# K stage spread out, first matrix copy ahead of the v store, u chunk loads one per weight unit, attention halves first in the first projection step

## The reference

```python
hn = rms_norm(h, norm1_g[l])                       # h: 272 tokens x 2048
q, k, v, u, g_na, g_ssm = jnp.split(hn @ w_in[l], IN_SPLITS, axis=-1)
y_na  = neighbourhood_attention(q, k, v, rpb) @ w_proj_na[l]
y_ssm = s5_branch(u, ...) @ w_proj_ssm[l]          # scan over positions, both directions, then GLU
mixed = sigmoid(g_na) * y_na + sigmoid(g_ssm) * y_ssm
h = h + mixed @ w_out[l]
h = h + conv_gated_ffn(rms_norm(h, norm2_g[l]), w_up[l], conv_w[l], conv_b[l], w_down[l])
return rms_norm(h, final_g)[:, N_META:]
```

## Time and profile before

| what | value |
|---|---|
| median of three runs | 1484.79 us (1483.28 to 1488.35) |
| the profiled execution | 1484.02 us, of which the profile's span is 1482.3 us |
| busy: PE / DVE / ACT / POOL | 1458.3 / 589.0 / 672.0 / 1032.8 us |
| granted TensorE clock, mean | 0.994 |
| DMA, mean over the span | 187 GB/s |

### The profile page before, as it was taken

One profiled execution on the slowest core, in us unless ns is written; L12 is line 12 of the kernel. 1 busy time (PEld: TensorE's weight loads), 2 busy tenths in 40 slices (PEclk: granted clock), 3 DMA queues, 4 the chain that ended last, 5 costly groups with the idle time before them and its releaser, 6 DMA issues.

```text
span 1482.3 us, 30668 instructions
## 1 busy us (share of the span) xinstructions
PE 1458.3 (98%) x11826; PEld 1384.7 (93%) x11826; DVE 589.0 (40%) x1159; ACT 672.0 (45%) x913; POOL 1032.8 (70%) x488
## 2 busy tenths in 40 slices
PE   8999999999999999999999999999999999999997
PEld 7999999999888999999999999999999998888886
DVE  3766888888546334533322222222222222003002
ACT  5536444442344364454554444444444443334333
POOL 5500038860577778888788888888888887888885
PEclk8999999999999999999999999999999999999999
DMA  7997457654676445575565555555555556555653
GB/s 211 301 206 223 140 158 221 195 176 121 171 226 206 150 159 176 182 257 178 169 193 185 184 184 183 180 181 181 183 182 184 184 183 197 187 186 184 194 187 130
DMA packets 250495, 277.14 MB, mean 187 GB/s; under 512 B 30749, under 2 KB 236925, under 8 KB 249773
## 3 DMA queue, kind: packets, MB, share of 16 engines
q1 hardware_dynamic: 235840, 254.84, 56.2%
q10 hardware_dynamic: 14508, 21.09, 4.4%
q0 software_dynamic: 64, 0.07, 0.0%
HBM read 263.32 MB, written 12.39 MB: 186 GB/s over the span
## 4 chain that ended last, share of the span: by engine, by line
PE 87%; DVE 4%; ACT 2%; DMA 2%; SPq 1%; issue 1%; DVEq 1%; POOL 0%; ACTq 0%; POOLq 0%
PE ps L1538 22%; PE ps L1540 21%; PE ps L1539 21%; PE ps L1906 6%; PE ps L1908 6%; PE ps L1907 6%; PE ps L1748 1%; DMA w_raw<-in_w_in 1%; DVE w_lo L524 1%; ACT w_hi L520 1%; SPq L462 1%; SPq L438 1%; PE ps L1754 0%; DVE w_nat L1192 0%; DMA x_tokens<-in_x 0%
## 5 line engine op out<-in xcount | busy, mean ns | idle before, releaser
L524 POOL TENSOR_TENSOR w_lo<-w_raw,w_hi 128x1024 fp32r<-128x1024 f32 x417 | 1001.9, 2409 | 369.0 <-ACT w_hi L520 230.5
L520 ACT ACTIVATE w_hi<-w_raw 128x1024 fp32r<-128x1024 f32 x464 | 489.9, 1060 | 673.1 <-PE ps L1540 483.8
L1538 PE MATMUL ps<-act_hi,w_hi 128*128 128x258 f32 (+2 forms) x2432 | 695.5, 286 | 2.2 <-DVE w_lo L524 1.3
L1540 PE MATMUL ps<-act_hi,w_lo 128*128 128x258 f32 (+2 forms) x2432 | 691.0, 284 | 0.0
L1539 PE MATMUL ps<-act_lo,w_hi 128*128 128x258 f32 (+2 forms) x2432 | 689.9, 284 | 0.0
L1538 PEld LDWEIGHTS ps<-act_hi,w_hi 128*128 128x128 f32 x2432 | 461.7, 190 | 7.8 <-issue 5.1
L1539 PEld LDWEIGHTS ps<-act_lo,w_hi 128*128 128x128 f32 x2432 | 462.4, 190 | 0.0
L1540 PEld LDWEIGHTS ps<-act_hi,w_lo 128*128 128x128 f32 x2432 | 460.9, 190 | 0.0
L1906 PE MATMUL ps<-w_hi,hidden_hi 128*128 128x512 f32 x352 | 139.2, 395 | 0.0
L1907 PE MATMUL ps<-w_hi,hidden_lo 128*128 128x512 f32 x352 | 139.0, 395 | 0.0
L1908 PE MATMUL ps<-w_lo,hidden_hi 128*128 128x512 f32 x352 | 139.0, 395 | 0.0
(11 more groups left out here) (268 smaller groups left out, 1551.7 us busy)
## 6 DMA issues: line engine op xcount, KB each, us to landing
w_raw<-in_w_up SPq DMA_DIRECT2D x176, 512.0 KB, 3.5
w_raw<-in_w_in SPq DMA_DIRECT2D x128, 512.0 KB, 4.2
w_raw<-in_w_down SPq DMA_DIRECT2D x88, 512.0 KB, 4.4
w_raw<-in_w_out SPq DMA_DIRECT2D x32, 512.0 KB, 3.4
w_raw<-in_w_proj_na SPq DMA_DIRECT2D x16, 512.0 KB, 3.3
w_raw<-in_w_proj_ssm SPq DMA_DIRECT2D x16, 512.0 KB, 3.4
w_raw<-in_w_glu SPq DMA_DIRECT2D x8, 512.0 KB, 3.4
bias_rows<-skew_scratch ACTq DMA_DIRECT2D x24, 128.0 KB
```

Source lines behind the costliest of these rows:

```text
L520: act.activation(slot(whi, k), slot(raw, k), ACT.Copy).then_inc(s_hi, 1)
L524: pool.tensor_tensor(slot(wlo, k), slot(raw, k), slot(whi, k).bitcast(F), ALU.subtract).then_inc(s_lo, 1)
L1538: mm(o, slot(whi, k)[:, cols], xh[:, kt, lo:lo + n], start=kt == 0, stop=False)
L1540: ins = mm(o, slot(wlo, k)[:, cols], xh[:, kt, lo:lo + n], start=False, stop=kt == units * UKT - 1)
```

## The change

Four edits, and one that follows from them in the weight order:

1. The parameter transposes on PE move from ahead of u unit 8 to between units 9 and 10 (`between=param_transposes`).
2. The eight `u_chunks` DMAs on SP are issued one behind each load of the last eight v units (24 to 31); the wait for the u stores stands behind the load of unit 24.
3. k stage. On ACT, `wt_copy(0)` now comes before the last v store and `hi_unit` 0 of the stage, and within each tile one high part is made between `s_copy` and `wt_copy`. On PE each tile is chunk_in, dense, w_trans, dense; the wait for `s_kev` stands behind `chunk_in` of odd tiles.
4. First projection step: both attention halves first (banks 0, 1 and 4, 5), then the wait for `s_zl`, then both scan halves. The weights are loaded in that order, and `mix_blocks(0)` waits for 6 and 8 units in place of 4 and 8.

```diff
             load_in(U_V, 2 * HALF, 0)
-            load_in(U_V, 2 * HALF, 1, range(3))
-            sp.wait_ge(s_ust, 16 * 4)
-            sp.wait_ge(s_crp, 1)
-            for g in range(2):
-                for j in range(CHUNK):
-                    sp.dma_start(U2[64 * g + GROUP * j:64 * g + GROUP * (j + 1), :, :],
...
-            load_in(U_V, 2 * HALF, 1, range(3, 8))
+            for k in range(8):
+                load_in(U_V, 2 * HALF, 1, (k,))
+                if k == 0:
+                    sp.wait_ge(s_ust, 16 * 4)
+                    sp.wait_ge(s_crp, 1)
+                g, j = k // CHUNK, k % CHUNK
+                sp.dma_start(U2[64 * g + GROUP * j:64 * g + GROUP * (j + 1), :, :],
...
-            with sp.Fori(0, 4) as i:
+            for k in range(8):
+                w = (w_proj_na, w_proj_ssm)[k // 4]
+                load(U_PROJ, k, kblock(w[0], (k % 4 // 2) * CB, k % 2))
+            with sp.Fori(1, 4) as i:
...
+            def v_store(i, k):
                 act.wait_ge(s_vcp, 2 * i + (k + 1 + SEED))
...
+            wt_copy(0)
+            v_store(ITERS_IN - 1, 1)
             hi_unit(act, U_K + DEPTH, 0)
-            wt_copy(0)
             hi_unit(act, U_K + DEPTH, 1)
...
             for t in range(KH):
                 s_copy(t)
+                if 2 * t + 2 < 16:
+                    hi_unit(act, U_K + DEPTH, 2 * t + 2)
                 if t + 1 < KH:
                     wt_copy(t + 1)
                 if t % 2 == 1:
                     store_block(t // 2)
-                for k in (2 * t + 2, 2 * t + 3):
-                    if k < 16:
-                        hi_unit(act, U_K + DEPTH, k)
+                if 2 * t + 3 < 16:
+                    hi_unit(act, U_K + DEPTH, 2 * t + 3)
...
-            def mix_blocks(i, mixed_lo, first):
+            def mix_blocks(i, mixed_lo, first, done):
                 for k in range(2):
-                    dve.wait_ge(s_used, 8 * i + (U_PROJ + 4 * (k + 1)))
+                    dve.wait_ge(s_used, 8 * i + (U_PROJ + done[k]))
...
+            mix_blocks(0, mxl[0], 0, (6, 8))
+            mix_blocks(1, mxl[0], 0, (4, 8))
...
-            product(U_U, 8, 4, hnh, hnl, 0, L, (0, 1))
+            product(U_U, 8, 4, hnh, hnl, 0, L, (0, 1), between=param_transposes)
...
-            chunk_in(0)
-            w_trans(1)
-            for t in range(1, KH):
-                if t % 2 == 0:
-                    pe.wait_ge(s_kev, t // 2)
-                dense(U_K + 2 * t, 0, L, 0)
-                if t % 2 == 1:
-                    dense(U_K + 2 * t + 1, 0, L, 0)
+            for t in range(KH):
                 chunk_in(t)
                 if t + 1 < KH:
+                    if t % 2 == 1:
+                        pe.wait_ge(s_kev, (t + 1) // 2)
+                    dense(U_K + 2 * t + 2, 0, L, 0)
                     w_trans(t + 1)
-                if t % 2 == 0:
-                    dense(U_K + 2 * t + 1, 0, L, 0)
+                    dense(U_K + 2 * t + 3, 0, L, 0)
...
-            with pe.Fori(0, 4) as i:
+            for k in range(2):
+                product(U_PROJ, 2 * k, 2, anh, anl, 0, NL, (4 * k, 4 * k + 1))
+            pe.wait_ge(s_zl, KH)
+            for k in range(2):
+                product(U_PROJ, 4 + 2 * k, 2, zh, zl, 0, NL, (4 * k + 2, 4 * k + 3))
+            with pe.Fori(1, 4) as i:
                 for k in range(2):
                     pe.wait_ge(s_mx, 4 * i + (2 * k - 2 + SEED))
                     product(U_PROJ + 8 * i, 4 * k, 2, anh, anl, 0, NL, (4 * k, 4 * k + 1))
-                    pe.wait_ge(s_zl, KH)
```

More of the change, by code:

```diff
@@ L432, in _ @@
             load_in(U_V, 2 * HALF, 0)
-            load_in(U_V, 2 * HALF, 1, range(3))
-            sp.wait_ge(s_ust, 16 * 4)
-            sp.wait_ge(s_crp, 1)
-            for g in range(2):
-                for j in range(CHUNK):
-                    sp.dma_start(U2[64 * g + GROUP * j:64 * g + GROUP * (j + 1), :, :],
-                                 u_d[:, :, j, :].rearrange("k (b g c) n -> g c (k b) n", b=PB, g=2)[g]).then_inc(s_u2, 16)
-            load_in(U_V, 2 * HALF, 1, range(3, 8))
+            for k in range(8):
[5 more added lines that the diff above has]
+                sp.dma_start(U2[64 * g + GROUP * j:64 * g + GROUP * (j + 1), :, :],
+                             u_d[:, :, j, :].rearrange("k (b g c) n -> g c (k b) n", b=PB, g=2)[g]).then_inc(s_u2, 16)
             sp.wait_ge(s_pad2, 16)
@@ L756, in v_blocks @@
                         v_copy(i, 0)
+                        v_store(i, 0)
                     elif i:
                         v_copy(i - 1, 1)
+                        v_store(i - 1, 1)
             for i in range(ITERS_IN):
@@ L1405, in mix_blocks @@
                                           ALU.subtract).then_inc(s_ml, 1)
-            with dve.Fori(0, 2) as i:
-                mix_blocks(i, mxl[0], 0)
+            mix_blocks(0, mxl[0], 0, (6, 8))
+            mix_blocks(1, mxl[0], 0, (4, 8))
             dve.wait_ge(s_gs, 4)
             with dve.Fori(2, 4) as i:
-                mix_blocks(i, mxl[1], KH)
+                mix_blocks(i, mxl[1], KH, (4, 8))
             dve.wait_ge(s_xre, 16)
@@ L1598, in _ @@
                     half_unit(U_U, 4 + q, q, 4, m, hnh, hnl, 0, L, 2 + m)
[L1600 to L1615, removed]
+            def param_transposes():
+                pe.wait_ge(s_par, 16 * 10)
+                pe.wait_ge(s_rows, 1)
+                pe.wait_ge(s_gcp, 1)
+                for n in range(2):
+                    nc.tensor.transpose(ps[:, 5, 88 * n:88 * (n + 1)], crow[:, n, :], ident[0:88, 0:88])
+                for h in range(2):
+                    nc.tensor.transpose(ps[:, 5, 4 * FT + h:4 * FT + h + 1], prs[0:1, WK * h:WK * h + P], ident[0:1, 0:1])
+                    nc.tensor.transpose(ps[0:NB, 5, 4 * FT + 2 + h:4 * FT + 3 + h], prs[0:1, WK * h + P:WK * (h + 1)],
+                                        ident[0:1, 0:1])
+                for t in range(2):
+                    nc.tensor.transpose(ps[:, 5, 4 * FT + 4 + t:4 * FT + 5 + t], prq[0:1, P * t:P * (t + 1)], ident[0:1, 0:1])
+                nc.tensor.transpose(ps[0:2, 5, 4 * FT + 6:4 * FT + 7], prq[0:1, SEQ:SEQ + 2], ident[0:1, 0:1])
+                for n in range(3):
+                    nc.tensor.transpose(ps[:, 7, P * n:P * (n + 1)], rows[:, n, :], ident[:, :])
+                nc.tensor.transpose(ps[:, 7, 3 * P:3 * P + PAIRS], drw2[:, :, :, :].rearrange("q g j c -> q (g j c)"),
+                                    ident[0:PAIRS, 0:PAIRS]).then_inc(s_ptp, 1)
```

## The result

The changed kernel takes 1477.17 us (median of 6 runs, 1475.88 to 1478.23); the kernel before took 1484.49 beside it (6 runs, 1481.66 to 1488.35). The ratio is 0.9949, 95% interval 0.9935 to 0.9962: 7.3 us faster. In a later comparison, 5 runs against 9, it was 0.9956 (0.9943 to 0.997), with a median of 1477.99. The forecast was 1481.4 in a range that began at 1477.5: the sign was right, and the gain is 2.2 times the 3.4 us forecast.

A forecast was written before the change was run, and what follows sets the result against it. PE was taken to bound the kernel, busy 1458.3 of 1482.3 us, losing time only in its waits; terms 1.3 + 0.0 + 0.7 + 1.4 = 3.4 us gave 1481.4 for the median, range 1477.5 to 1486.5 (own case 1479.3 to 1483).

The forecast's parts named there:

- That is the ceiling of the gain.: Whole kernel: the five PE waits the change can touch sum to 6.9 us, 0.46% of the time, the most it can gain.
- Parameters, 0.0: Parameter transposes moved later: the 1.0 us wait goes but is handed back at unit 21; bounds 1.0 gained, 0.3 lost.
- a slack of about 1 us at unit 21: Low part of unit 21 ready at 94.2 against PE's start at 94.25; moved up by 1.0, PE would wait there.
- u chunks, -1.3: u chunk DMAs spread one per unit: two PE waits for low parts go, 1.3 us gained; bounds 1.3 or 0.
- k stage, -0.7: New k stage order: 1.5 and 1.1 us of waits go, 1.2 of breaks and 0.7 of new wait come; 0.7 gained.
- The new wait: k stage behind chunk_in(1): PE waits 0.7 us for k_block(0), as the v store moves behind the w_tr copy; bounds 0, 1.2.
- The breaks: k stage, tiles 1 to 7: seven more breaks between dense runs on PE at 0.17 us each, 1.2 us lost.
- Projection, -1.4: First projection step: the 2.0 us z_lo wait goes, a 0.6 wait comes at unit 8; 1.4 gained, bounds 2.0 and -0.4.
- Everything behind is bound by PE, so it lasts to the end: After the edited places: the summed gain of 3.4 us is kept to the kernel's end.
- The rival of contended additions: First projection step: DVE's additions run into POOL and take 2.61 us, gain 1.65, time 1483.1 us; chance 0.13.
- Nothing is given back: Rival, whole kernel: no new waits, all 6.9 us gained, or 5.7 with breaks paid; put at 1478.5 us; chance 0.23.
- A gain above 7 us: Whole kernel: stated sign that, like a loss with none of the forecast waits, would make the whole reading wrong.

The follow-up runs named there:

- the single parts: Four runs, each one part of the change alone on the kernel before: parameters 1484.2 us, u chunks 1483.79, k stage 1479.74, projection 1481.64.
- load_first: Kernel before, from the third attention step ACT rounds attention halves and issues the next loads ahead of the first weight split; 1480.37 us, ratio 0.9973.
- store_first: Changed kernel with the last v store back ahead of the first matrix copies on ACT's queue; 1476.28 us, ratio 0.9951 to the kernel before.
- copy_late: Changed kernel with POOL's copy of c_rows held back to about where it ran in the kernel before; 1476.31 us, one run.
- after_again: Changed kernel repeated unaltered, on one chip beside the kernel before (1483.97 us); 1477.99 us, 5 runs.
- the part alone: Kernel before with only the parameter transposes moved to after two units of the next product; 1484.2 us, 10 runs, ratio 0.9999.

## Why the prediction was wrong

- **"That is the ceiling of the gain."** This step failed first. The sum of waits, 6.9 us, is no ceiling where idling also costs clock: the table of the kernel before had a mean granted clock of 0.994, and the sum put it at nothing. In the 24 places where one of the four waits stands in a profile of this case (the two kernels, the single parts, load_first, store_first, copy_late and after_again), 12 are followed by a fall; at the three waits that the change removes it is 8 of 15. Three places by 8/15 by 1.5 us is 2.4; the mean clocks of the runs (0.9939 in 60, 0.9956 in 11) at 1.19 per 0.001 give 2.0. At equal clock, by that line, the changed kernel stands 4.7 us under the one before (standard error 0.5): that is what the prediction's terms had to sum to, and they summed to 3.4. The 1.52 at the fourth scores in the table is the same effect but not the change's: that wait is in both kernels, and the profiles of after_again and store_first have a fall there.
- **Parameters, 0.0.** The mechanism, a slack of about 1 us at unit 21, was right and its size off: the later chain was taken up to the last by gaps that I counted as 4.0 of 5.05 (the chain itself came 4.6 later), and POOL's copy moved off the four multiplications, so unit 21's low part came 1.02 earlier. The trace gives 1.23. The ten times of the part alone, at equal clock, give 0.2 (0.5): whether all 1.23 reaches the end is open.
- **u chunks, -1.3.** Right in kind; 1.75 and 1.74 in two traces. Stops cost 0.1 to 0.25 us more than the list shows: parameters 1.05 listed and 1.22 gained, w_tr 1.54 and 1.60, here 1.25 in two and 1.74. The list counts idle time, not the overlap of neighbouring matmuls that a stop breaks: behind the stop at 149.08 the second matmul starts 0.23 us after the first, in a dense run 0.13.
- **k stage, -0.7.** The new wait was found, and under-sized: 1.46, not 0.7. DVE's first copy, held by the store, started 2.1 us behind the end of the first chunk_in, not 1.4 (the store's second half landed 5.1 us after its issue, not 4.0), and chunk_in(1) came 0.2 sooner. The breaks were over-sized: 64.90 us from the first chunk_in to the last is 64.43 less 1.1 of w_nat waits plus 1.46 and 0.1. So seven breaks cost 0.1, not 1.2. I had added up the durations of runs (2.0, 3.20, 0.85, 3.20) where the starts in the earlier trace rows and above overlap: the dense run begins 1.93 behind the chunk_in's start and lasts 3.13. The Trainium skill, page TensorE: Matmul & The Clock Gate, section Part 3: Packing small matmuls, whose rule on weight loads pulled ahead I weighed and set aside, came out nearer than my row. Sum of the trace: 1.1. That it is near the 0.7 forecast is luck: the breaks were 1.1 too dear and the wait 0.8 too cheap.
- **Projection, -1.4.** Right at its place: additions uncontended at 0.77, a wait of 0.58 at unit 8, and 1.45 gained up to the second norm in the changed kernel's first trace. But "Everything behind is bound by PE, so it lasts to the end" failed here: in three of five traces with the edit a wait of 1.2 for mixed_lo_b takes the gain back (217.58 to 217.64 us against 217.62). The rival of contended additions didn't come where it was looked for; DVE beside POOL came at the end of the mixing. That the first trace shows the 1.4 is in part luck.
- **The rivals.** "Nothing is given back" came nearest in time (1478.5), but not for its reason: the waits behind chunk_in(1) and at unit 8 were both there. A gain above 7 us was named as what would make the reading wrong, and it did: the largest part that was wrong is the clock.

## What to carry to other kernels

Before a sum of waits is made, look at the granted clock behind each long wait of the engine that bounds the kernel, and at the spread of mean clocks over the runs: a wait of 1.5 to 2 us can cost its length and, in some executions only, nearly as much again. Compare kernels at equal clock, or over many runs, before a microsecond is given to an edit. Take the price of a break from start to start, not from the durations of rows that overlap. And follow a gain past its own stage, in more than one trace: the 1.4 us of the projection were gone some 80 us later in three traces of five.

## What the runs showed of the hardware that was not expected

- PE waits of 1.05 to 2.6 us were followed by 3.4 us at a granted clock of 0.5 in half of the cases, with the same code and the same wait. For v_tail_ring the four of 2.0 to 2.6 us were, the five of 1.2 to 1.7 were not; the 1.05 at the parameters was in two of five. What decides it was not found.
- Such a fall cost 1.52 us at two places of the kernel, in four traces (14.95 to 16.47 us, 217.62 to 219.13 or 219.14 us).
- Multiplying ones during such waits kept the clock at 1.0 from the start's fall to PE's last work in the one trace taken.
- A DVE instruction of 0.23 us took 1.84 beside one POOL copy, and two low parts of the mixing took 5.15 us beside POOL's, where one takes 0.41 with POOL idle.
- The v store landed 4.0 and 5.1 us after its two issues in the changed kernel, 3.7 and 4.8 in store_first, where the kernel before had 3.0 and 4.0.
